# A hybrid decoder layer on eight cores: scratch in the staging tiles' layout, ones rows kept in the rings, and the first FFN norms spread among the gates

## The chip, the cores and the metric

The kernel runs on the eight cores of one Trainium2 chip. Core c works on sequence c//2 and on one half of its chunks (the odd or the even ones); no core waits for another. The time is that of the slowest core, in microseconds of the device. On each core five engines run their own in-order queues: TensorE (PE in the profile), ScalarE (ACT), VectorE (DVE), GpSimd (POOL) and SyncE (SP, which issues most of the DMAs).

## What is computed

One decoder layer on x of 4 x 8192 x 1024, cut to what matters:

```python
h = rmsnorm(x, g_mix_pre)
a_val, a_gate, q, k, v, f_logit = split(h @ w_in)          # 512 channels each, 8 heads for f
u = causal_depthwise_conv(a_val * sigmoid(a_gate))         # width 31
conv_out = silu(layernorm(u))
c = cumsum(log_sigmoid(f_logit + b_forget))                # per head
logits = q @ k.T / 8 + c[query] - c[key]                   # causal, 8 heads of 64
attn_out = softmax(logits) @ v
x = x + rmsnorm(concat(conv_out, attn_out) @ w_out, g_mix_post)
h = rmsnorm(x, g_ffn_pre)
y = (silu(h @ w_gate) * (h @ w_up)) @ w_down               # d_ff 2816
x = x + rmsnorm(y, g_ffn_post)
```

## The kernel before

**Chunks and streams.** A sequence has 16 chunks of 512 tokens. A core owns 8 of them (index j) and makes keys and values of all 16, of two chunks for each j. Three streams of work are recorded one into another by a small planner: `p_stream` (norms, K, V, Q, GLU gates, depthwise conv; until about 950 us), `f_stream` (output projection A1, first norm A2, second norm A3, then the FFN's up and down blocks; until the end), and `a_stream`, the attention, of which the planner mixes a share into both. The order of all instructions on each engine is fixed when the program is built: the planner counts the cost of what it has recorded (`fa`), and draws attention steps at a rate of at most 0.6 of the other work. A `yield ("att", d)` draws attention steps of d us by its own costs at that place, and they count against later ones.

**Dependencies.** Every operation names keys that it reads and writes (L77 on, `_record`). A DMA that writes a key waits for the last writer of that key and for its readers. Where that writer is another DMA, the wait stands on the issuing engine's queue, ahead of the instruction, until the earlier transfer has landed. The helpers `ld` (L345) and `st` (L349) give the keys of the whole buffer: `keys = buf.keys if keys is None else keys`. The key and value rings and the query rings are single-key buffers.

**Scratch.** K, V, q and the decay terms of a chunk pass through scratch tensors in device memory. Part 1 stores K twice: all of it in `k2_s` (per head 128 rows, key blocks of two halves on rows 0 to 63 and 64 to 127), and the half that the diagonal needs once more in `kd_s`, whose 68 rows per head hold 64 of K, one of ones and three of decay. `q_s` has 64 rows of q, one of decay, three of ones. Four stores at the start fill the ones rows.

**Attention loads.** A head (j, h) needs `s_qr` (q with its extra rows), `s_qw` (q again, on partitions 64 to 127) and `s_kd`; a unit (j, h, u) needs `s_kr` (K of chunk pair u) and `s_vr`. Heads have rings of `NQ = 3`, units of `NKV = 4`. `a_pump` (L1048) issues in turn the next head and the next unit as far as rings are free and stores are recorded, after each finished unit. All of these loads, the weights' loads of the FFN (`w_pump`), and the stores of K, q, V, u and conv stand on SP's one queue in that order; only the loads of x and u, and the conversion of the weights, are issued by POOL.

**First FFN norms.** `f_stream` (L989) at its start runs the conv's layernorm, gates 0 and 1 of the last own chunk (32 matmuls on `s_winG`), then A1(0) (64 matmuls on `s_wout`), A2(0) (whose statistics are two matmuls that read `s_hlA`), gates 2 and 3, A3(0) (two more of these matmuls), and attention of 3.0. Between the two statistics lie a chain on the other engines: the reciprocal root on ACT, eight residual steps of two instructions on DVE (L884, L886), eight squares, and their sum on POOL (L412, L428).

## Time and profile before

| | us |
|---|---|
| median of three runs (slowest core) | 2553.92 |
| the runs, from to | 2546.47 to 2798.3 |
| time of the profiled execution | 2545.8 |
| its span, core 6, the slowest | 2544.2 |
| spans of cores 0 to 7 | 2528.3, 2506.9, 2506.8, 2525.8, 2519.6, 2540.4, 2544.2, 2524.4 |
| PE busy | 2281.6 (90%) |
| ACT busy | 1576.0 (62%) |
| DVE busy | 1058.6 (42%) |
| POOL busy | 542.2 (21%) |
| DMA packets, bytes | 252408, 390.70 MB |

The span is that of the slowest core in one profiled execution; 1.6 us of its time lie outside of it. All cores do the same amount of work on the same addresses of their own, so differences between them are waits. SPq in a row is SP issuing a DMA; "landing" is the time from that issue to the last byte's arrival. "x16" counts instructions.

### The profile page before, as it was taken

Reading aid. Unit: us, or ns where it says so; the run is one execution under the profiler, and the core shown is the slowest. Engines: PE = TensorE matmul, PEld = TensorE weight load, DVE = VectorE, ACT = ScalarE, POOL = GpSimd, SP = SyncE. Lnnn points to the kernel's source line nnn. Section 1 sums busy time; section 2 is a strip of 40 time slices with the busy share of each in tenths; the row PEclk is TensorE's granted clock in tenths of the full one; section 3 lists DMA queues with packets and bytes.
Section 4 is the critical chain, followed back from the end, with each engine's and each line's share of the span. In section 5 each row is a group of like instructions: output and inputs, shape, how many; then the busy total and the mean of one; then the engine's idle time right before and its main releaser. Section 6 shows DMA issues by size and latency. Waiting matters only on the chain.

```text
span 2544.2 us, 52937 instructions; the slowest of 8 cores (2506.8 to 2544.2 us)
## 1 busy us (share of the span) xinstructions
PE 2281.6 (90%) x19680; PEld 1044.7 (41%) x19680; DVE 1058.6 (42%) x1640; ACT 1576.0 (62%) x1393; POOL 542.2 (21%) x901
## 2 busy tenths in 40 slices
PE   6888888889799869898999999999999999999895
PEld 2343334344344424344444444444444444444342
DVE  3545454434344443342424424424424342443643
ACT  2166566767577566676677777777767767772311
POOL 0231222121121240132023113113102202302301
PEclk9998899999899989999999999999999999998997
DMA  6996769597755956757635554654663463553542
GB/s 144 199 160 147 164 140 185 118 177 162 130 144 112 205 133 150 188 120 199 194 115 152 176 161 127 187 171 114 180 193 98 142 212 109 147 164 120 169 144 91
DMA packets 252408, 390.70 MB, mean 154 GB/s; under 512 B 29856, under 2 KB 182688, under 8 KB 252032
## 3 DMA queue, kind: packets, MB, share of 16 engines
q1 hardware_dynamic: 218928, 302.99, 43.9%
q0 software_dynamic: 33232, 84.34, 16.4%
q8 instruction: 164, 2.69, 0.5%
q14 instruction: 84, 0.69, 0.1%
HBM read 352.02 MB, written 77.20 MB: 169 GB/s over the span
## 4 chain that ended last, share of the span: by engine, by line
PE 65%; ACT 11%; issue 7%; DVE 6%; DMA 5%; SPq 3%; POOL 2%; DVEq 0%; ACTq 0%; POOLq 0%
PE pbig L375 65%; ACT s_pt L1097 5%; DMA s_kr<-k_s 2%; DVE s_tmp L884 2%; SPq L347 2%; DMA s_xs<-xT 1%; SPq L350 1%; ACT L387 1%; DVE s_x L886 1%; ACT s_sq L481 1%; ACT s_rstd L387 1%; ACT s_pt L1102 1%; DVE s_hT L468 1%; POOL s_ssA L412 1%; POOL s_pt L1106 1%
## 5 line engine op out<-in xcount | busy, mean ns | idle before, releaser
L1097 ACT ACTIVATE s_pt<-pbig,s_bias 128x2048 bf16<-128x2048 f32 x512 | 1005.7, 1964 | 448.1 <-PE pbig L375 445.3
L375 PE MATMUL pbig<-s_h,s_wr 128*128 128x512 bf16 x2816 | 694.3, 382 | 10.7 <-DVE s_sa L932 10.1
L375 PEld LDWEIGHTS pbig<-s_vr,s_pt 128*128 128x128 bf16 x8832 | 348.4, 98 | 174.1 <-issue 56.5
L375 PE MATMUL pbig<-s_vr,s_pt 128*128 128x65 bf16 x8832 | 369.9, 195 | 27.8 <-issue 8.6
L375 PE MATMUL pbig<-s_qr,s_kr 64*128 64x512 bf16 x1024 | 314.3, 387 | 81.3 <-ACT s_pt L1097 49.1
L375 PEld LDWEIGHTS pbig<-s_h,s_wr 128*128 128x128 bf16 x2816 | 243.7, 98 | 331.6 <-issue 112.5
L932 DVE SCALAR_TENSOR_TENSOR s_sa<-s_th,pbig 128x512 f32<-128x512 f32 x176 | 120.8, 686 | 488.1 <-ACT s_th L931 488.1
L375 PE MATMUL pbig<-s_qw,s_kr 64*128 64x512 bf16 x1024 | 315.7, 389 | 0.5 <-DMA s_qw<-q_s 0.5
L1106 POOL TENSOR_SCALAR_AFFINE_SELECT s_pt<-s_pt 128x128 bf16<-128x128 bf16 x256 | 86.5, 338 | 948.1 <-ACT s_pt L1102 922.8
L375 PE MATMUL pbig<-s_actA,s_wr 128*128 128x512 bf16 x1024 | 257.2, 381 | 1.7 <-DVE s_mix L965 1.1
L412 POOL TENSOR_TENSOR s_ssA<-s_ssA,s_sqr 128x512 f32<-128x512 f32 x112 | 153.0, 1366 | 449.3 <-ACT s_sqr L405 445.0
L375 PEld LDWEIGHTS pbig<-s_qr,s_kr 64*128 64x128 bf16 x1024 | 58.9, 94 | 293.2 <-issue 292.7
L375 PE MATMUL pbig<-s_hT,s_winKV 128*128 128x512 bf16 x512 | 146.0, 423 | 22.2 <-DVE s_hT L468 13.0
L931 ACT ACTIVATE s_th<-pbig 128x512 f32<-128x512 f32 x176 | 104.0, 591 | 87.3 <-PE pbig L375 82.1
L375 PE MATMUL pbig<-s_hT,s_winG 128*128 128x512 bf16 x512 | 134.6, 398 | 7.6 <-DVE s_ust L755 4.3
L375 PEld LDWEIGHTS pbig<-s_actA,s_wr 128*128 128x128 bf16 x1024 | 90.8, 98 | 122.6 <-issue 39.0
L375 PE MATMUL pbig<-s_winKV,s_hT 128*128 128x8 bf16 (+1 forms) x1024 | 139.7, 275 | 1.1 <-DVE s_vst L792 1.1
L412 POOL TENSOR_TENSOR s_ssV<-s_ssV,s_sqr 128x512 f32<-128x512 f32 x53 | 70.3, 1326 | 267.3 <-ACT s_sqr L405 267.1
L1102 ACT ACTIVATE s_pt<-pbig 128x1280 bf16<-128x1280 f32 x64 | 79.0, 1235 | 65.0 <-PE pbig L375 65.0
L884 DVE TENSOR_TENSOR s_tmp<-s_mix,s_rstd 128x512 f32<-128x512 f32 x120 | 97.6, 813 | 51.3 <-ACT s_rstd L389 51.3
L886 DVE SCALAR_TENSOR_TENSOR s_x<-s_tmp,s_vecs,s_x 128x512 f32<-128x512 f32 x120 | 112.0, 933 | 13.2 <-DVE s_tmp L884 0.5
L468 DVE SCALAR_TENSOR_TENSOR s_hT<-s_xs,s_vecs,s_rstd 128x512 bf16<-128x512 f32 x128 | 91.1, 745 | 34.9 <-ACT s_rstd L389 34.9
...
## 6 DMA issues: line engine op xcount, KB each, us to landing
...
s_wr<-wd_b SPq DMA_DIRECT2D x128, 352.0 KB, 3.2
s_vr<-v_s SPq DMA_DIRECT2D x288, 130.0 KB, 3.7
...
```

Source lines behind the costliest of these rows:

```text
L347: P.dma(q, lambda e: e.dma_start(out=out, in_=in_), reads=reads, writes=keys, sem=sem or buf.name)
L375: P.op("pe", lambda e: e.matmul(out, lhsT=lhsT, rhs=rhs, start=start, stop=stop, **kw), reads=reads, writes=[wkey])
L387: P.op("act", lambda e: e.activation(out=r[:, 0:ncol], in_=pb[b][:, 0:ncol], func=AF.Ln, bias=epsb[:, 0:1], scale=scale), reads=[PB(b)] + ...
L412: P.op(eng, lambda e: e.tensor_tensor(out=ss[:], in0=ss[:], in1=d[:], op=ALU.add), reads=ss.keys + d.keys, writes=ss.keys)
L468: return lambda: P.op("dve", lambda e: e.scalar_tensor_tensor(out=dst[:, k, :], in0=src[:, k, :], scalar=V(goff + k), in1=r[:], op0=ALU.mu ...
L884: P.op("dve", lambda e: e.tensor_tensor(out=T[:], in0=src[:, ob, :], in1=rstd[:], op=ALU.mult), reads=[src.keys[ob]] + rstd.keys, writes=T ...
L886: P.op("dve", lambda e: e.scalar_tensor_tensor(out=X[:, ob, :], in0=T[:], scalar=V(goff + ob), in1=X[:, ob, :], op0=ALU.mult, op1=ALU.add) ...
L931: P.op("act", lambda e: e.activation(out=T[:], in_=pb[bg][:], func=AF.Tanh, scale=0.5), reads=[PB(bg)], writes=T.keys)
L932: defer("ff", [lambda: P.op("dve", lambda e: e.scalar_tensor_tensor(out=A[:], in0=T[:], scalar=1.0, in1=pb[bg][:], op0=ALU.add, op1=ALU.mult),
L1097: P.op("act", lambda e: e.activation(out=p[:], in_=pbig[:, 0:4, :], func=AF.Exp, bias=bias[:, c, h:h + 1], scale=1.0), reads=bk + bias.key ...
L1102: P.op("act", lambda e: e.activation(out=p[:].rearrange("p a t -> p (a t)")[:, 0:1280], in_=pbig[:, 0:3, :].rearrange("p a t -> p (a t)")[ ...
L1106: P.op("pool", lambda e, ap=ap: e.affine_select(out=ap, in_=ap, pattern=[[1, 128]], base=0, channel_multiplier=-1, compare_op=ALU.is_ge, f ...
```

## The change

**Scratch.** `k2_s` and `kd_s` give way to one `k_s` (own index, 128 partitions, 4 head pairs, 2 halves, 512 tokens), whose row is what one partition of the staging tile holds: one store of 8 KB runs instead of eight. q, decay and V get tensors laid out in the same way (`q_s`, `c_s`, `v_s`), with one store each; the second copy of the diagonal half of K is no longer made. V's staging tiles grow to 12 blocks, so that the decayed copies lie in place, and `vst2` goes away; three small buffers of the conv's halo move behind `vst0`.

**Ones rows.** Six memsets on DVE fill rows 64 to 67 of the q and kd rings once; the four stores of ones are gone. A head is now loaded by five DMAs (q, its decay row, q again, kd, its three decay rows), K of a unit by two of 64 partitions each, with a semaphore each; V by one as before.

**First norms.** In `f_stream` A1(0) now comes ahead of the gates; gate 0 stands between A1 and A2, gates 1, 2 and 3 with attention of 1.0 behind each, and 2.0 more, between A2 and A3.

```diff
--- before.py
+++ after.py
@@ -208,12 +208,10 @@
     m32_d = dt_in("m32", [128, 32])
     yT_d = nc.dram_tensor("yT", [NOWN, 128, 8, CH], F32, kind="ExternalOutput").ap()
     scr = lambda name, shape: nc.dram_tensor(name, shape, BF16).ap()
-    k2_s = scr("k2_s", [NH, 128, S // 2])
-    kd_s = scr("kd_s", [NH + 1, 68, NOWN * CH])
-    q_s = scr("q_s", [NH + 1, 68, NOWN * CH])
-
-    kf, qf_ = kd_s.rearrange("h r t -> (h r) t"), q_s.rearrange("h r t -> (h r) t")
-    v_s = scr("v_s", [NH, 128, NOWN, 12, 65])
+    k_s = scr("k_s", [NOWN, 128, 4, 2, CH])
+    q_s = scr("q_s", [NOWN, 128, 4, CH])
+    c_s = scr("c_s", [NOWN, 4, 4, NH, 128])
+    v_s = scr("v_s", [128, NOWN, NH, 12 * 65])
     attn_s = scr("attn_s", [DATT, NOWN * CH])
     conv_s = scr("conv_s", [DCONV, NOWN * CH])
     u_s = scr("u_s", [NOWN, DCONV, UW])
@@ -301,10 +299,9 @@
     cst = BP("cst", [128, 128], BF16)
 
     OV = lambda name, shape, dt, over, parts=1, d=0: Buf(name, shape, dt, parts, [over.off + d])
-    vst = [OV("vst0", [128, NH, 8, 65], BF16, w4), OV("vst1", [128, NH, 8, 65], BF16, tmp[0])]
-    vst2 = OV("vst2", [128, NH, 4, 65], BF16, tmp[0], 1, 8320)
+    vst = [OV("vst0", [128, NH, 12, 65], BF16, w4), OV("vst1", [128, NH, 12, 65], BF16, tmp[0])]
     ust.append(OV("ust2", [128, CH], BF16, hlA, 1, 1024))
-    assert hlA.off + 1024 >= vst2.off + vst2.size and vst2.off >= vst[1].off + vst[1].size
+    assert hlA.off + 1024 >= vst[1].off + vst[1].size
 
     wout = Buf("wout", [128, 8, D], BF16, cur=[winKV.off], planes=4)
     mix = OV("mix", [128, 8, CH], F32, u4, 8)
@@ -556,23 +553,15 @@
 
         def decay(tb):
             def f():
-                o, ok = (W[:, :, 4 + tb, :], W.keys) if tb < 4 else (vst2[:, :, tb - 4, :], vst2.keys)
-                i_ = W[:, :, 4 + tb, :] if tb < 4 else W[:, :, tb - 4, :]
+                o, i_ = W[:, :, 4 + tb, :], W[:, :, tb + (4 if tb < 4 else -4), :]
                 P.op("dve", lambda e: e.tensor_tensor(out=o, in0=i_, in1=et3[:, tb, :].unsqueeze(2).to_broadcast([128, NH, 65]), op=ALU.mult),
-                     reads=W.keys + et.keys, writes=ok)
+                     reads=W.keys + et.keys, writes=W.keys)
             return f
-
-        def st_v():
-            st("sp", v_s[:, :, j, 0:8, :].rearrange("h p b d -> p h (b d)"), W[:].rearrange("p h b d -> p h (b d)"), W.keys, [("v_s", j, 0)], W.name)
-            st("sp", v_s[:, :, j, 8:12, :].rearrange("h p b d -> p h (b d)"), vst2[:].rearrange("p h b d -> p h (b d)"), vst2.keys, [("v_s", j, 1)], "vst2")
 
         def part4():
             flush("st")
-            for a in range(3):
-                st("sp", kd_s[0:NH, 65 + a, j * CH:(j + 1) * CH].rearrange("h (b t) -> b h t", t=128),
-                   cst[32 * a:32 * a + 32, :], cst.keys, [("c_s", j, a)], ("cst", a))
-            st("sp", q_s[0:NH, 64, j * CH:(j + 1) * CH].rearrange("h (b t) -> b h t", t=128), cst[96:128, :], cst.keys, [("c_s", j, 3)], ("cst", 3))
-            st_v()
+            st("sp", c_s[j].rearrange("a b h t -> (a b h) t"), cst[:], cst.keys, [("c_s", j)], "cst")
+            st("sp", v_s[:, j, :, :].rearrange("p h b -> p (h b)"), W[:].rearrange("p h b d -> p (h b d)"), W.keys, [("v_s", j)], W.name)
             ready[2 * j] = ready[2 * j + 1] = True
 
         nop = lambda: None
@@ -677,7 +666,7 @@
     u4h = (Buf("xh", [128, 8, HN], F32, 1, hcur), Buf("hh", [128, 8, HN], BF16, 8, hcur), Buf("sqh", [128, 8, HN], BF16, 8, hcur),
            None)
     assert hcur[0] <= u4.off + u4.size
-    hcur = [acc.off]
+    hcur = [vst[0].off + vst[0].size + 31 & ~31]
     u4h = u4h[:3] + (Buf("uh", [128, 4, HN], BF16, 1, hcur),)
     cwb = Buf("cwb", [128, 8, 16], F32, 1, hcur)
     m32 = Buf("m32", [128, 32], F32, 1, hcur)
@@ -696,9 +685,10 @@
         ld("sp", kmask, kmask[:], kmask_d)
         P.op("pool", lambda e: e.memset(ones_f[:], 1.0), writes=ones_f.keys)
         P.op("dve", lambda e: e.memset(carry[:], 0.0), writes=carry.keys)
-        P.op("dve", lambda e: e.memset(pt[0][:, 0:2, :], 1.0), writes=pt[0].keys)
+        for t in qring + kdring:
+            P.op("dve", lambda e, t=t: e.memset(t[64:68, :], 1.0), writes=t.keys)
         for W in vst:
-            P.op("dve", lambda e, W=W: e.memset(W[:, :, :, 64:65], 1.0), writes=W.keys)
+            P.op("dve", lambda e, W=W: e.memset(W[:, :, 0:8, 64:65], 1.0), writes=W.keys)
         P.op("dve", lambda e: e.tensor_scalar(out=V(V_HG, 8), in0=V(V_LNG, 8), scalar1=0.5, scalar2=None, op0=ALU.mult),
              reads=vecs.keys, writes=vecs.keys)
         norm_sq(0)
@@ -710,11 +700,6 @@
         yield from norm_fin(1)
         flush("h")
         load_x(2)
-        one = pt[0][0:96, 0:2, :].rearrange("p a t -> p (a t)")
-        st("sp", kd_s[0:NH, 64, :].rearrange("h (s t) -> h s t", t=1024), one[0:32, :], pt[0].keys, [("one", 0)], "one0")
-        st("sp", kd_s[NH, 0:12, :].rearrange("r (s t) -> r s t", t=1024), one[0:48, :], pt[0].keys, [("one", 2)], "one2")
-        st("sp", q_s[NH, 0:12, :].rearrange("r (s t) -> r s t", t=1024), one[0:48, :], pt[0].keys, [("one", 3)], "one3")
-        st("sp", q_s[0:NH, 65:68, :].rearrange("h r (s t) -> h r s t", t=1024), one, pt[0].keys, [("one", 1)], "one1")
         yield from p_kv(1)
         yield from norm_fin(2)
         flush("h")
@@ -772,14 +757,7 @@
                 yield from norm_fin(i + 2, i + 3)
 
         def st_k():
-            two = lambda t, o: t.rearrange("(hp two) r t -> two r hp t", two=2)[o]
-            for o in range(2):
-                K = kst[64 * o:64 * o + 64]
-                for a in range(2):
-                    st("sp", two(k2_s[:, 64 * a:64 * a + 64, j * CH:(j + 1) * CH], o), K[:, :, a, :, :].rearrange("p h b t -> p h (b t)"),
-                       kst.keys, [("k2", j, o, a)], ("kst", o, a))
-                    st("sp", two(kd_s[0:NH, 0:64, j * CH + 256 * a:j * CH + 256 * a + 256], o), K[:, :, a, 1, :],
-                       kst.keys, [("kd", j, o, a)], ("kstd", o, a))
+            st("sp", k_s[j].rearrange("p c a t -> p (c a t)"), kst[:].rearrange("p c a b t -> p (c a b t)"), kst.keys, [("k_s", j)], "kst")
         if own:
             defer("st", [st_k], 4)
         W, V0 = vst[min(j, 1)], 0 if own else 4
@@ -825,9 +803,7 @@
                 norm_sq(i + (1 if i == 3 else 2))
 
         def st_q():
-            for o in range(2):
-                st("sp", q_s[0:NH, 0:64, :].rearrange("(hp two) d t -> two d hp t", two=2)[o, :, :, j * CH:(j + 1) * CH],
-                   qst[64 * o:64 * o + 64, :, :], qst.keys, [("q_s", j, o)], ("qst", o))
+            st("sp", q_s[j].rearrange("p c t -> p (c t)"), qst[:].rearrange("p c t -> p (c t)"), qst.keys, [("q_s", j)], "qst")
             q_ready[j] = True
         defer("st", [st_q], 4)
         if not last:
@@ -994,14 +970,15 @@
         H = hT[(NCH - 1) % 3]
         bulk_flush("wo")
         yield from conv_ln(J - 1)
-        for cb in range(2):
-            yield from gates(J, cb, H)
         flush("c")
         yield from A1(0, range(8))
+        yield from gates(J, 0, H)
         yield from A2(0)
         w_pump()
-        for cb in range(2, 4):
+        for cb in range(1, 4):
             yield from gates(J, cb, H)
+            yield ("att", 1.0)
+        yield ("att", 2.0)
         yield from A3(0)
         yield ("att", 3.0)
         for j in range(NOWN):
@@ -1052,12 +1029,12 @@
                 j, h = heads[qn[0]]
                 if ready[2 * j + 1] and q_ready[j]:
                     r, w, kd = qring[qn[0] % NQ], qtwin[qn[0] % NQ], kdring[qn[0] % NQ]
-                    t = slice(j * CH, (j + 1) * CH)
-                    rq = [("q_s", j, 0), ("q_s", j, 1)]
-                    ld("sp", r, r[:], qf_[h * 68:h * 68 + 80, t], reads=rq + [("c_s", j, 3), ("one", 1), ("one", 3)])
-                    ld("sp", w, w[64:128, :], q_s[h, 0:64, t], reads=rq)
-                    ld("sp", kd, kd[:], kf[h * 68:h * 68 + 80, t],
-                       reads=[("kd", j, o, a) for o in range(2) for a in range(2)] + [("c_s", j, a) for a in range(3)] + [("one", 0), ("one", 2)])
+                    d = slice(64 * (h % 2), 64 * (h % 2) + 64)
+                    ld("sp", r, r[0:64, :], q_s[j, d, h // 2, :], reads=[("q_s", j)])
+                    ld("sp", r, r[67:68, :], c_s[j, 3:4, :, h, :], reads=[("c_s", j)], sem=r.name + "c")
+                    ld("sp", w, w[64:128, :], q_s[j, d, h // 2, :], reads=[("q_s", j)])
+                    ld("sp", kd, kd[0:64, :].rearrange("p (a t) -> p a t", a=2), k_s[j, d, h // 2, :, 256:512], reads=[("k_s", j)])
+                    ld("sp", kd, kd[64:67, :].rearrange("p (b t) -> p b t", b=4), c_s[j, 0:3, :, h, :], reads=[("c_s", j)], sem=kd.name + "c")
                     qn[0] += 1
                     did = True
             if un[0] < len(units) and un[0] < uf[0] + NKV:
@@ -1065,9 +1042,11 @@
                 if ready[2 * u + 1] and ready[2 * j + 1]:
                     kr, vr = kring[un[0] % NKV], vring[un[0] % NKV]
                     n = CH if u < j else CH // 2
-                    ld("sp", kr, kr[:, 0:n], k2_s[h, :, u * CH:u * CH + n], reads=[("k2", u, o, a) for o in range(2) for a in range(2)])
+                    d = slice(64 * (h % 2), 64 * (h % 2) + 64)
+                    for a in range(2):
+                        ld("sp", kr, kr[64 * a:64 * a + 64, 0:n], k_s[u, d, h // 2, a, 0:n], reads=[("k_s", u)], sem=(kr.name, a))
                     b0 = 4 if u < j else 0
-                    ld("sp", vr, vr[:], v_s[h, :, u, b0:b0 + 8, :], reads=[("v_s", u, 0)] + [("v_s", u, 1)] * (u < j))
+                    ld("sp", vr, vr[:].rearrange("p b d -> p (b d)"), v_s[:, u, h, b0 * 65:b0 * 65 + 520], reads=[("v_s", u)])
                     un[0] += 1
                     did = True
             if not did:
```

**The order on SP, the first attention loads.** Rows of the instruction order on SP before, where `a_pump` first runs: `s_kr`, `s_vr` and the numbers are ring buffers, and what stands in brackets is the semaphore that SP waits for ahead of the row.

```order
L347 DMA s_kr_49<-k_s 128x256
L347 DMA s_vr_53<-v_s 128x520 [waits p_ds_36]
L347 DMA s_qr_60<-q_s 80x512
L347 DMA s_qw_63<-q_s 64x512
L347 DMA s_kd_66<-kd_s 80x512
L347 DMA s_kr_50<-k_s 128x256
L347 DMA s_vr_54<-v_s 128x520
```

The same place after the change; each `p_ds` semaphore named here is that of the DMA in the row above, which writes the same buffer:

```order
L344 DMA s_qr_60<-q_s 64x512
L344 DMA s_qr_60<-c_s 1x4x128 [waits p_ds_39]
L344 DMA s_qw_63<-q_s 64x512
L344 DMA s_kd_66<-k_s 64x2x256
L344 DMA s_kd_66<-c_s 3x4x128 [waits p_ds_42]
L344 DMA s_kr_50<-k_s 64x256
L344 DMA s_kr_50<-k_s 64x256 [waits p_ds_44]
L344 DMA s_vr_54<-v_s 128x520
```

Sixteen issues in a row without a wait have become a queue in which the second half of each K load, and the decay rows of q and of kd, wait until the DMA ahead of them into that buffer has landed. There are 288 such waits for K and 128 for the heads in the program.

**The order on PE, ahead of A3(0).** Rows on PE before, up to the second statistics (`s_hlA`); `s_winG` are gate matmuls, the pairs of `s_qr` and `s_qw` with `s_kr` are attention scores of a unit, `s_kd` those of a diagonal, `s_vr` the values:

```order
L375 MATMUL pbig<-s_qr_59,s_kd_65 128x128
L375 MATMUL pbig<-s_qr_59,s_kd_65 128x256
L375 MATMUL pbig<-s_hT_80,s_winG 128x512 x4
L375 MATMUL pbig<-s_vr_54,s_pt_57 128x65 x16
L375 MATMUL pbig<-s_hT_80,s_winG 128x512 x4
L375 MATMUL pbig<-s_qr_60,s_kr_51 128x512
L375 MATMUL pbig<-s_qw_63,s_kr_51 128x512
L375 MATMUL pbig<-s_qr_60,s_kr_51 128x512
L375 MATMUL pbig<-s_qw_63,s_kr_51 128x512
L375 MATMUL pbig<-s_hlA,s_ones_bf 128x512 x2
```

And after:

```order
L372 MATMUL pbig<-s_identb,s_atok_71 128x128 x4
L372 MATMUL pbig<-s_qr_60,s_kr_52 128x512
L372 MATMUL pbig<-s_qw_63,s_kr_52 128x512
L372 MATMUL pbig<-s_qr_60,s_kr_52 128x512
L372 MATMUL pbig<-s_qw_63,s_kr_52 128x512
L372 MATMUL pbig<-s_vr_55,s_pt_58 128x65 x16
L372 MATMUL pbig<-s_qr_60,s_kr_52 128x512
L372 MATMUL pbig<-s_qw_63,s_kr_52 128x512
L372 MATMUL pbig<-s_qr_60,s_kr_52 128x512
L372 MATMUL pbig<-s_qw_63,s_kr_52 128x512
L372 MATMUL pbig<-s_vr_56,s_pt_57 128x65 x16
L372 MATMUL pbig<-s_hlA,s_ones_bf 128x512 x2
```

Between the two statistics stood 32 gate matmuls, three rounds of score matmuls off the diagonal and one on it; now 48 gate matmuls, seven rounds and one.

## Rows read from the trace of the kernel before

**Rows 1.** The page: the chain that ended last, by engine and line.

```profile
PE 65%; ACT 11%; issue 7%; DVE 6%; DMA 5%; SPq 3%; POOL 2%; DVEq 0%; ACTq 0%; POOLq 0%
PE pbig L375 65%; ACT s_pt L1097 5%; DMA s_kr<-k_s 2%; DVE s_tmp L884 2%; SPq L347 2%; DMA s_xs<-xT 1%; SPq L350 1%; ACT L387 1%; DVE s_x L886 1%; ACT s_sq L481 1%; ACT s_rstd L387 1%; ACT s_pt L1102 1%; DVE s_hT L468 1%; POOL s_ssA L412 1%; POOL s_pt L1106 1%
```

**Rows 2.** Waits of PE, core 6: releaser, us in total, times, longest.

```profile
PE pbig L375 <- POOL s_hlA L428: 17.8, 3, 12.3
PE pbig L375 <- DMA s_kr<-k_s: 17.8, 5, 7.0
PE pbig L375 <- issue: 17.1, 4, 6.6
```

**Rows 3.** Tile s_h, cores 1 and 6: ns min/median/max, first and last start.

```profile
L375 PE MATMUL pbig<-s_h,s_wr x2816: 376/379/634, 917.8 to 2440.4; 128*128 128x512 bf16 x188
...
L375 PE MATMUL pbig<-s_h,s_wr x2816: 376/379/634, 959.4 to 2477.8; 128*128 128x512 bf16 x188
```

**Rows 4.** Timeline of SP, core 6, first attention loads: start us, us, issue.

```profile
132.35 0.35 SPq L347 DMA_DIRECT2D s_qr<-q_s  x1
...
141.48 0.43 SPq L347 DMA_DIRECT2D s_vr<-v_s  x1
142.01 0.38 SPq L350 DMA_DIRECT2D u_s<-s_ust  x1
```

**Rows 5.** Tile s_kr, 130 to 199 us: own chunk 0's score matmuls.

```profile
L375 PE MATMUL pbig<-s_qr,s_kr x16: 376/386/603, 144.1 to 198.4; 64*128 64x512 bf16 x16
```

**Rows 6.** K loads' landing, core 6, windows 130:180, 334:540, 900:1000, 1200:1600.

```profile
DMA to landing us min/median/max: 5.7/8.3/12.6
...
DMA to landing us min/median/max: 2.1/5.7/22.2
...
DMA to landing us min/median/max: 2.4/3.0/5.1
...
DMA to landing us min/median/max: 2.0/3.6/7.9
```

**Rows 7.** K loads issued for own chunks 1 to 4: ns each, first, last.

```profile
L347 SPq DMA_DIRECT2D s_kr<-k_s x16: 337/521/2697, 186.0 to 332.4; - x16
...
L347 SPq DMA_DIRECT2D s_kr<-k_s x24: 320/522/2860, 335.9 to 538.1; - x24
...
L347 SPq DMA_DIRECT2D s_kr<-k_s x32: 319/442/4189, 546.0 to 818.4; - x32
...
L347 SPq DMA_DIRECT2D s_kr<-k_s x40: 319/428/7257, 820.9 to 1153.2; - x40
```

**Rows 8.** Timeline of SP's queue, core 6, behind the store burst of chunk 5.

```profile
648.73 6.95 SPq L347 DMA_DIRECT2D s_qr<-q_s  x1
...
657.36 4.19 SPq L347 DMA_DIRECT2D s_kr<-k_s  x1
```

**Rows 9.** DMA queue 1, 640:680, then 2320:2480: packets, MB, share of 16 engines.

```profile
q1 hardware_dynamic: 3811, 3.01, 50.7%
...
q1 hardware_dynamic: 7098, 22.37, 45.2%
```

**Rows 10.** Timeline of PE, core 6: the two statistics of the first norms.

```profile
921.98 0.58 PE L375 MATMUL pbig<-s_hlA,s_ones_bf 128*128 128x512 bf16 x1 [3.54 <-POOL s_hlA L428]
...
948.61 0.59 PE L375 MATMUL pbig<-s_hlA,s_ones_bf 128*128 128x512 bf16 x1 [12.26 <-POOL s_hlA L428]
```

**Rows 11.** Page, section 5: the gate matmuls (x512), busy us and mean ns.

```profile
L375 PE MATMUL pbig<-s_hT,s_winG 128*128 128x512 bf16 x512 | 134.6, 398 | 7.6 <-DVE s_ust L755 4.3
```

**Rows 12.** Waits and timeline of SP in the FFN stage, core 6.

```profile
SPq L163 <- PE pbig L375: 1216.7, 461, 14.4
...
1699.81 0.32 SPq L347 DMA_DIRECT2D s_kr<-k_s  x1
1705.00 0.32 SPq L347 DMA_DIRECT2D s_vr<-v_s  x1
```

**Rows 13.** Timeline of PE, core 6: the longest wait for a K load.

```profile
679.40 0.58 PE L375 MATMUL pbig<-s_qr,s_kr 64*128 64x512 bf16 x1 [6.98 <-DMA s_kr<-k_s]
```

## The prediction

> **What bounds the kernel now.** I read the page first, and in it the chain that ended last: two thirds of it are matmuls, and the largest item of a DMA is the wait for K loads, with SP's issues behind it [rows 1]. So PE sets the time, and a transfer matters where PE stands still for it. The list of PE's waits tells how much that is: 17.8 us on K loads, 17.1 us put down to "issue", in four pieces of up to 6.6 us, which I take to be loads too, and 17.8 us on the split of the sum of squares, nearly all of it at two places [rows 2, 10]. Next I compared cores. From the first FFN matmul on, cores 1 and 6 run alike (1522.6 and 1518.4 us to the last); before it core 6 is 41.6 us later [rows 3]. All that differs between cores lies in the first 960 us, where chunks are projected and stored. There the loads are slow: K lands after 8.3 us (median) in the first attention stretch, after 5.7 us between 334 and 540 us, but after 3.0 us in the quiet 900 to 1000 us and 3.6 us in the FFN stage [rows 6]. Behind a store burst the issue of a load alone takes 4.19 to 6.95 us [rows 8], and PE then waits up to 6.98 us for K [rows 13].
>
> **What the stores give.** One store per tensor replaces ten issues of K and q and six of decay and V, half a megabyte per chunk is not written twice, and rows grow to 8 KB. In the burst, queue 1 moves 3.01 MB in 3811 packets (0.79 KB each) with 50.7% of 16 engines over 40 us, which is 85 ns a packet and 9.3 GB/s an engine; with the weights' 3.15 KB packets it is 45.2% over 160 us for 22.37 MB, 163 ns and 19 GB/s [rows 9]. So long rows move about twice as fast, and bursts should at least halve. The ends of the gain are 0 (the two waits stay) and the 41.6 us by which core 6 lies behind core 1 [rows 3]; the K and issue waits sum to 34.9 us [rows 2]. I take 30. The Trainium skill ("DMA: Bandwidth & Descriptors", Specifications) puts the least transfer for full rate at 512 B, which the old rows already had; by that page the longer rows give nothing and the sum below would be 30 us higher. The trace speaks against it, with 9.3 and 19 GB/s on either side [rows 9].
>
> **What the loads cost.** The order on SP shows it: the second half of each K load waits for the landing of the first, and so do the decay rows of q and of kd, since they write one key. These are 288 and 128 landings, and everything on SP stands behind each. With L the time from issue to landing, and the issues at 0.35 to 0.5 us [rows 4], a unit now takes SP L + 0.8, a head 2L + 1.3. Before, three heads and four units went out from 132.35 to 141.91 us [rows 4], without a wait. Per stage:
> - own chunk 0 (8 heads, 8 units): 24L + 17, where SP had 66 us from the first issue to the last use [rows 4, 5];
> - chunk 1: 32L + 23 in the 150 us from its first K load to that of chunk 2 [rows 7];
> - chunk 2: 40L + 30 in 210; chunk 3: 48L + 36 in 275; chunk 4: 56L + 42 in some 334, its end with the FFN's weights.
>
> L is not in the trace: no load of half the rows, alone on its queue, is shown. Its ends are 2.4 us, the fastest quiet load, and 8.3 us, the first stretch [rows 6]. That 8.3 has four units in flight at once; now one transfer of SP is in flight, but xT and the weights' conversion share the engines. I take 4.5, nearer to the quiet 3.0 and the FFN's 3.6 than to the crowded stretch. Then chunk 0 takes 125 us for 66, 59 late; chunk 1 167 for 150, 17 late; chunks 2 to 4 fill 100, 92 and 88% of SP's time, and what bunches there (a head and two units after one release, stores between) I put at 8 us each, 24 in all, between 0 and 60. The stores of u, decay and V behind the first loads come late too, and the gates wait for their staging tiles; that falls into the same standstill. In the FFN stage SP waits 1216.7 us for PE over the run, and the next V load goes out 5.2 us after its K load, when PE frees the value buffer [rows 12]: a wait of 3.6 us for the first half ends inside it. I take 5 for the heads and weights there, between 0 and 40. Together 105.
>
> The Trainium skill (the same page, Rules for kernel authors) says of two transfers to disjoint partition halves: "Don't bother — they serialize", since both use the same 16 engines, and asks for one transfer of 128 partitions. That speaks against this edit, and by it the split has no gain to set against the waits; nothing is in the sum for one.
>
> **The first norms.** PE stands still for 3.54 us ahead of A2's statistics and for 12.26 us ahead of A3's [rows 10]. Between the two now lie 16 more gate matmuls, 6.4 us at 398 ns [rows 11], and four more rounds of scores with their values. That is enough to cover both, but attention drawn here is missing later. I take a gain of 10, between 3 and 15.8. In return A1(0) comes 32 gate matmuls earlier, 12.7 us, and may meet its weights and the last attention output on their way: 3, between 0 and 12.7.
>
> **Small things.** The four stores of ones and a memset go, six memsets of four rows come: nothing, since DVE is not in that place's wait. V's decay in place and the moved halo buffers change no instruction's size: nothing, unless a buffer is freed later, for which I have 5 as an upper end. After a stall matmuls take 0.58 us for the median's 0.38 [rows 3, 13]; some 40 of them after new stalls are 8 us, between 0 and 20.
>
> **The sum.** 2545.8 (the profiled execution) + 105 − 30 − 10 + 3 + 8 = 2621.8 us. The profiled time is 8.1 below the median of the runs, 2553.92, and no correction is made for that. 2% of the median, about what can be told from no change, is 51 us: faster ends at 2502.8, slower begins at 2605.0.
>
> **The rivals.**
> - **Half-loads land quickly, and the costs and gains cancel.** At L = 3.8 chunk 0 is 42 late, chunk 1 nothing (145 of 150), bunching 15 and the clock 4: 2545.8 + 42 + 15 + 4 − 30 − 10 + 3 = 2570. For it: a load of half as many rows, with smaller bursts beside it. Against: 5.7 and 8.3 in just these stretches [rows 6]. This ends and slower begins at L of about 4.3.
> - **The gain alone shows; faster.** One mechanism: the first half has landed by the time that SP would have had to wait for PE in any case, as in the FFN stage [rows 12], and the first stage keeps up. For 24L + 17 to fit into 66 us, L has to be 2.1 or less; at 2.4 it is 9 late. With that gone, the store term at its upper end and the norms at 10: 2545.8 − 41.6 − 10 + 3 = 2497; it decides at L of about 2.2. For it: loads have landed in 2.0 to 2.1 us now and then [rows 6]. Against: those are minima.
> - **The bursts stay.** The stores give nothing, as K still goes out in one piece ahead of the loads and holds the rings as long; then 2622 + 30 = 2652. Against it are the packet times [rows 9]. It is what the 512 B of the Trainium skill ("DMA: Bandwidth & Descriptors", Specifications) would make of the longer rows.
> - **The change doesn't do what it says for the norms.** The chain behind A2 is as long as before, and PE meets it later; 2632 instead of 2622. It is inside the forecast's range.
>
> **How the numbers follow.** I give the forecast 0.45, the bursts that stay 0.11, cancelling 0.34 and the gain alone 0.10. The predicted time is the first's, 2622. Its own range goes from 2605 to 2720: at L = 5.5 chunks 0 to 4 are 83, 49, 40, 25 and 16 late, 213 in all against 76, with the other terms 2748, and I go most of the way. The whole range has to take in most of the cancelling case, 2530 to 2605, and the lower end of that is where L is 3.0 (23 + 10 late, no clock; 2545.8 + 33 − 40 + 3 = 2542, less some 12 for the store term's other end). So 2530 to 2720. Slower is 0.45 + 0.11 = 0.56, same 0.34, faster 0.10.
>
> **What would show it.** In the new profile SP's waits have a row of DMA `s_kr`, `s_qr` and `s_kd` landings, some 416 in all, over 1000 us together; the first K load of chunk 1 goes out at about 250 instead of 186 us; PE has stalls behind DMA or "issue" between 144 and 330 us that sum to 60 or more; the first FFN matmul of core 6 is later than 959 us by 50 to 80, and cores lie closer together; from there to the end nothing changes by over 15 us; the 12.26 us at A3's statistics is below 6. The prediction is wrong if the new waits on SP last under 3 us each in the first 330 us, if PE doesn't wait there, or if the FFN stage becomes longer, which would mean that weights and stores behind the waits matter there too.

## The result, and the profile after

The change makes the kernel slower by far more than forecast: 2864.75 us, median of four runs, against 2565.54 for the kernel before on the same chip; ratio 1.1185, 95% interval 1.1076 to 1.1295. Forecast was 2622, with 2530 to 2720 as the range. The profiled execution took 2874.26 us, and its cores 2837.5 to 2871.7. Ratios here compare undisturbed runs only, while medians take in all; where the two differ, the ratio counts. The rows below are those of core 6, as before, unless another is named.

The chain that ended last, from the page (core 0), by engine and by line:

```profile
DMA 40%; PE 35%; SPq 11%; issue 5%; ACT 4%; DVE 4%; POOL 1%; DVEq 0%; ACTq 0%; POOLq 0%
PE pbig L372 35%; DMA s_kr<-k_s 23%; SPq L344 9%; DMA s_qr<-q_s 9%; DMA s_kd<-k_s 6%; ACT s_pt L1076 2%; DVE s_tmp L860 1%; SPq L347 1%; DMA s_cv<-conv_s 1%; DVE s_x L862 1%; ACT L384 0%; DMA s_xs<-xT 0%; DVE s_hT L465 0%; ACT s_rstd L384 0%; DMA wd_b<-w_down 0%
```

In [rows 1] matmuls were 65% and K loads 2% of it. Now DMA landings are 40% and the loads' issues by SP 9%: the path no longer runs along PE but along SP's queue and what it waits for. SP's own waits say it directly (releaser, us in total, times, longest):

```profile
SPq L161 <- DMA s_kr<-k_s: 1039.6, 288, 11.2
SPq L161 <- DMA s_qr<-q_s: 238.4, 64, 9.7
SPq L163 <- PE pbig L372: 189.4, 78, 10.1
SPq L161 <- DMA s_kd<-k_s: 182.9, 64, 10.5
```

These are the 416 landings of the prediction, 288 and twice 64, 1460.9 us together. What SP waited for PE has fallen from 1216.7 us [rows 12] to 189.4: over most of the run it is no longer PE that sets SP's pace. PE's waits now:

```profile
PE pbig L372 <- DMA s_kr<-k_s: 179.5, 47, 10.8
...
PE pbig L372 <- DMA s_cv<-conv_s: 40.2, 5, 13.9
...
PE pbig L372 <- DVE s_ust L740: 23.7, 3, 20.0
...
PE pbig L372 <- DMA s_qr<-c_s: 11.8, 4, 5.7
...
PE pbig L372 <- POOL s_hlA L425: 2.0, 1, 2.0
```

K loads cost PE 179.5 us where they cost 17.8 [rows 2]; the conv outputs' load for A1 (`s_cv`), behind the waits in the same queue, another 40.2, the u stores (through their staging tiles `s_ust`) 23.7, of which 20.0 in one piece. POOL's part of the wait for the split of the squares, 17.8 us before [rows 2], is down to 2.0. Where in the run it was lost is told by the first and last FFN matmul:

```profile
L372 PE MATMUL pbig<-s_h,s_wr x2816: 376/379/634, 1106.3 to 2785.8; 128*128 128x512 bf16 x188
```

The first comes at 1106.3 us for 959.4, so 146.9 of core 6's loss lie ahead of it; from there to the last one it is 1679.5 us for 1518.4 [rows 3], another 161.1. And a single landing isn't slow. For all K loads, issue to landing:

```profile
DMA to landing us min/median/max: 2.0/3.0/11.6
```

The median is 3.0 us, that of the quiet stretch before, where the first stretch had 8.3 [rows 6].

### The profile page after: what moved, and what is told of

Same layout as the page of the kernel before. It is cut to its first block, busy times and chain, and to the rows that moved or that the text cites. A ratio compares the mean times of both kernels' runs of the same rounds, so it can differ in the third digit from the quotient of the medians.

```text
span 2871.7 us, 53550 instructions; the slowest of 8 cores (2837.5 to 2871.7 us)
## 1 busy us (share of the span) xinstructions
PE 2356.3 (82%) x19680; PEld 1068.8 (37%) x19680; DVE 1066.8 (37%) x1645; ACT 1578.2 (55%) x1393; POOL 539.9 (19%) x901
## 3 DMA queue, kind: packets, MB, share of 16 engines
q0 software_dynamic: 33232, 84.34, 14.3%
## 4 chain that ended last, share of the span: by engine, by line
DMA 40%; PE 35%; SPq 11%; issue 5%; ACT 4%; DVE 4%; POOL 1%; DVEq 0%; ACTq 0%; POOLq 0%
PE pbig L372 35%; DMA s_kr<-k_s 23%; SPq L344 9%; DMA s_qr<-q_s 9%; DMA s_kd<-k_s 6%; ACT s_pt L1076 2%; DVE s_tmp L860 1%; SPq L347 1%; DMA s_cv<-conv_s 1%; DVE s_x L862 1%; ACT L384 0%; DMA s_xs<-xT 0%; DVE s_hT L465 0%; ACT s_rstd L384 0%; DMA wd_b<-w_down 0%
## 5 line engine op out<-in xcount | busy, mean ns | idle before, releaser
L372 PE MATMUL pbig<-s_h,s_wr 128*128 128x512 bf16 x2816 | 714.2, 391 | 18.2 <-DVE s_sa L908 17.5
L372 PE MATMUL pbig<-s_qr,s_kr 64*128 64x512 bf16 x1024 | 324.3, 397 | 287.3 <-DMA s_kr<-k_s 221.4
L372 PEld LDWEIGHTS pbig<-s_vr,s_pt 128*128 128x128 bf16 x8832 | 358.5, 100 | 173.6 <-issue 62.8
L372 PE MATMUL pbig<-s_vr,s_pt 128*128 128x65 bf16 x8832 | 379.6, 197 | 17.3 <-DVE s_atok L1116 8.5
L372 PE MATMUL pbig<-s_qw,s_kr 64*128 64x512 bf16 x1024 | 325.9, 400 | 2.7 <-DMA s_qw<-q_s 2.7
L912 DVE SCALAR_TENSOR_TENSOR s_actA<-s_sa,pbig 128x512 bf16<-128x512 f32 x128 | 87.7, 685 | 63.0 <-PE pbig L372 54.1
```

What stands on the lines that cost most here:

```text
L372: P.op("pe", lambda e: e.matmul(out, lhsT=lhsT, rhs=rhs, start=start, stop=stop, **kw), reads=reads, writes=[wkey])
L912: P.op("dve", lambda e: e.scalar_tensor_tensor(out=actT(f), in0=A[:], scalar=0.5, in1=pb[bu][:], op0=ALU.mult, op1=ALU.mult), reads=A.keys ...
```

## The experiments

All times are medians in us; a ratio is to the kernel before, run on the same chip. The last two columns are core 6's first FFN matmul in the profiled run, and the time from there to its last one.

| run | what it is | time | ratio (95%) | first FFN | FFN |
|---|---|---|---|---|---|
| before | | 2565.54 | 1 | 959.4 | 1518.4 |
| the change | | 2864.75 | 1.1185 (1.1076 to 1.1295) | 1106.3 | 1679.5 |
| e1 | no waits on landings | 2523.88 | 0.9841 (0.9778 to 0.9905) | 926.6 | 1520.4 |
| e2 | K waits only | 2637.35 | 1.0273 (1.0205 to 1.0341) | 992.0 | 1576.2 |
| e9 | head waits only | 2605.09 | 1.0148 (1.0083 to 1.0214) | 997.1 | 1527.2 |
| e3 | waits for own chunks 4 to 7 | 2725.25 | 1.0601 (1.0506 to 1.0696) | 955.3 | 1686.9 |
| e5 | waits for own chunks 0 to 3 | 2669.88 | 1.0469 (1.0401 to 1.0536) | 1085.0 | 1515.4 |
| e6 | all waits, V between the K halves | 2784.09 | 1.0882 (1.0804 to 1.0961) | 1069.0 | 1620.4 |
| e8 | before, with split K loads | 2781.12 | 1.062 (1.0523 to 1.0718) | 1045.0 | 1580.8 |
| e4 | no waits, K as one transfer | 2544.35 | 0.993 (0.9902 to 0.9958) | 930.0 | 1516.4 |
| e7 | e1 with the old norms' order | 2571.55 | 0.9892 (0.9811 to 0.9973) | 916.2 | 1524.8 |
| e10 | e4 with K by head in scratch | 2522.44 | 0.9855 (0.9803 to 0.9906) | 918.2 | 1515.0 |
| e11 | before, with the new norms' order | 2557.07 | 0.9995 (0.9962 to 1.0028) | 967.9 | 1518.1 |

e1, e4, e7 and e10 lie below both kernels, by 0.7 to 1.6%, and none of their intervals reaches 1.

**e1, the waits taken away.** The rings of K, q and kd get a second key for the second transfer, and each load writes its own (of q and kd the decay rows have the second); PE, which reads both keys, waits for both landings. No transfer, address or size changes.

```diff
-    kring = [B(f"kr{i}", [128, CH], BF16) for i in range(NKV)]
+    kring = [B(f"kr{i}", [128, CH], BF16, planes=2) for i in range(NKV)]
...
-                        ld("sp", kr, kr[64 * a:64 * a + 64, 0:n], k_s[u, d, h // 2, a, 0:n], reads=[("k_s", u)], sem=(kr.name, a))
+                        ld("sp", kr, kr[64 * a:64 * a + 64, 0:n], k_s[u, d, h // 2, a, 0:n], reads=[("k_s", u)], sem=(kr.name, a), keys=[kr.keys[a]])
```

> Every transfer of the changed kernel stays, but the two halves of a K load, and q or kd and their decay rows, have a key each, so the 416 waits of SP on landings are gone. Theory W (the waits hold up all that stands behind them on SP): the whole loss goes and the gains of stores and norms show, 2490 to 2540 us. Rival D (the transfers themselves: halves of 64 partitions, 256 B rows, 288 + 128 more of them, or the new layout's addresses): the loss stays for the most part, above 2750 us. A time between, 2600 to 2700, would mean that both count.

Measured 2523.88: the whole loss of some 340 us was the waits, and without them the change is 1.6% faster than the kernel before (0.95 to 2.2%). Theory W holds; D, by which halves of 64 partitions and 256 B rows would be dear in themselves, falls, since all of them are still there.

**e2 and e9, one kind of wait at a time.** Each has half of e1's edit: in e2 q and kd have two keys and K has one, in e9 K has two (`planes=2`, `keys=[kr.keys[a]]`) and q and kd one.

> Only the 288 K waits stay (1053 of 1494 us of landing waits in the changed kernel's profile), the 128 of the heads are gone. Theory W as a saturated queue: SP needs about 5.1 us a unit and 3 a head, 293 us for own chunk 5 where the stage lasted 318, so SP keeps up but for bunches and the time falls by far more than the heads' share of the waits: 2560 to 2640. Theory W as latency (each wait costs PE its share): 2865 - 0.3 x 340 = 2760. D: 2830 or more.

> The counterpart of the second run: only the 128 head waits stay (441 of 1494 us), the 288 K waits are gone. If loss is proportional to wait: 2523.9 + 0.3 x 341 = 2625. If it is what SP cannot absorb (theory W as a filled queue): SP needs 1.5 us a unit and 10 a head, about 150 us for own chunk 5 where the stage lasts 318, so only own chunks 0 and 1 are short of time: 2530 to 2565. The two halves would then cost 113 and some 20 apart and 341 together.

e2 at 2637 is within what the filled queue gives, with 113 us over e1. (The expectation's 5.1 us a unit and 3 a head give 269 us for own chunk 5 and not 293; either is less than the 318 of the stage.) e9 is a miss: 2605, some 80 us over e1, where 10 to 40 were expected. Its first and last FFN matmul show where:

```profile
L372 PE MATMUL pbig<-s_h,s_wr x2688: 376/379/634, 997.1 to 2524.3; 128*128 128x512 bf16 x192
```

From 997.1 to 2524.3 are 1527.2 us, 6.8 more than in e1: in the FFN stage the head waits cost next to nothing, as expected. All else, 70.5 us, lies ahead of it, where heads follow each other after one to four units and SP has to bring many of them at once. The first V load of own chunk 1 goes out 47 us later than in e1 (235.9 for 188.6), that of chunk 2 58 later (392.6 for 334.2): most of the loss is chunk 0's. So the place was foreseen and the size was not. Together 113 and 80 would be 193; the change lost 341. The two kinds don't add, as they would not if each uses up slack that the other needs; the count of one stage below bears that out.

**e3 and e5, one stage at a time.** The same keys as in e1, but where the condition holds both loads write both keys, and so the second waits: `j >= 4` in e3, `j < 4` in e5 (q, kd and their decay rows in the same way).

```diff
-                        ld("sp", kr, kr[64 * a:64 * a + 64, 0:n], k_s[u, d, h // 2, a, 0:n], reads=[("k_s", u)], sem=(kr.name, a))
+                        ld("sp", kr, kr[64 * a:64 * a + 64, 0:n], k_s[u, d, h // 2, a, 0:n], reads=[("k_s", u)], sem=(kr.name, a), keys=kr.keys if j >= 4 else [kr.keys[a]])
```

> All waits stay for own chunks 4 to 7 (attention from about 820 us on), none for chunks 0 to 3. In the prediction's working the FFN stage hides them, which gives 2520 to 2560. By the profile after, in which the first FFN matmul is some 160 us later and the rest another 160 us longer, it is 2660 to 2700, with the first FFN matmul of the slowest core below 980 us.

> The counterpart of the third run: waits for own chunks 0 to 3 only (80 units, 32 heads), none for 4 to 7. Theory W with the prediction's stage formula at the landing that the profile after shows (about 3.7 us of wait a landing): chunk 0 about 50 late, chunk 1 some 20, then bunching: the first FFN matmul some 80 to 130 us later than without waits, 2600 to 2650. If the two halves of the loss simply add to the full loss (341 us, of which the FFN's half was 201): 2523.9 + 140 = 2664. The FFN stage itself as without waits (about 1522 us from first to last FFN matmul).

e3 is the run that decides against the prediction's step, by which it would have taken 2520 to 2560; it also lies above the 2660 to 2700 that the profile after had led to. With waits only from own chunk 4 on, the first FFN matmul of core 6 comes at 955.3 us, 28.7 after e1's (chunk 4 starts at about 800 us, so part of that is chunk 4's), and the FFN takes 1686.9 us for 1520.4. e5 is the mirror: 1085.0, and an FFN of 1515.4. Its first FFN matmul is 158 us later than e1's where the stage formula gave 80 to 130, and 2670 is above the formula's 2600 to 2650, next to the 2664 of a plain sum. By the ratios e3 loses 7.6% of the kernel before's time to e1 and e5 6.3%, the change 13.4%: 13.9 for 13.4. Stage by stage the losses add; kind by kind, 4.3% and 3.1% for the same 13.4, they do not.

**e6, the same waits with V's issue inside.** One line moved: the V load goes out between the two K halves.

```diff
+                    b0 = 4 if u < j else 0
                     for a in range(2):
                         ld("sp", kr, kr[64 * a:64 * a + 64, 0:n], k_s[u, d, h // 2, a, 0:n], reads=[("k_s", u)], sem=(kr.name, a))
-                    b0 = 4 if u < j else 0
-                    ld("sp", vr, vr[:].rearrange("p b d -> p (b d)"), v_s[:, u, h, b0 * 65:b0 * 65 + 520], reads=[("v_s", u)])
+                        if a == 0:
+                            ld("sp", vr, vr[:].rearrange("p b d -> p (b d)"), v_s[:, u, h, b0 * 65:b0 * 65 + 520], reads=[("v_s", u)])
```

> The changed kernel with all 416 waits, but the V load of a unit is issued ahead of the second K half instead of behind it, so its issue of about 0.5 us falls into the wait. Nothing else moves. If SP's time is what bounds the kernel (theory W, saturated queue): 288 x 0.5 = 144 us of SP time less over a stage that SP fills, so 80 to 150 us faster than the change, 2715 to 2785. If what costs is the length of each load's chain (two landings one after the other): V comes a little earlier, K as late as before, 2840 to 2865. D: no change.

2784 is 81 us faster than the change, 77 by the ratios (1.0882 for 1.1185): at the edge of the lower range and clear of the rival's 2840. All 416 waits are there still, and K's second half goes out no sooner after its first, 4.2 us on average in both runs; what got shorter is SP's time for a unit. V comes earlier too, which the rival priced at 0 to 25 us. So most of the gain is SP's time.

**e8, the split alone.** The kernel before, with each K load in two halves that write one key.

```diff
-                    ld("sp", kr, kr[:, 0:n], k2_s[h, :, u * CH:u * CH + n], reads=[("k2", u, o, a) for o in range(2) for a in range(2)])
+                    for a in range(2):
+                        ld("sp", kr, kr[64 * a:64 * a + 64, 0:n], k2_s[h, 64 * a:64 * a + 64, u * CH:u * CH + n], reads=[("k2", u, o, a) for o in range(2)], sem=(kr.name, a))
```

> The kernel before, whole, with one edit: each K load is issued as two transfers of 64 partitions that write one key, so 288 landing waits on SP and no other part of the change. W: as in the second run, where these waits cost 113 us over the run without them, and more since the store bursts are still there: 2660 to 2720. If the cost came from the new layout together with waits: 2600 or less.

Ratio 1.062: on the 2549.22 of the kernel before on its chip that is 2707, within the expected range, and 158 us of loss. So the waits need nothing of the new scratch to cost what they do; with the new scratch the same 288 cost 113 (e2). Why they cost less there isn't shown; the expectation put it down to the store bursts.

**e4 and e10, K in one transfer.** Without waits the split itself may still cost. e4 joins the halves by an access:

```diff
-                    for a in range(2):
-                        ld("sp", kr, kr[64 * a:64 * a + 64, 0:n], k_s[u, d, h // 2, a, 0:n], reads=[("k_s", u)], sem=(kr.name, a))
+                    ld("sp", kr, kr[:, 0:n], k_s[u, d, h // 2, :, 0:n].rearrange("p a t -> a p t"), reads=[("k_s", u)])
```

e10 joins them by another layout of the scratch, into which K is stored by four DMAs of 64 x 4 x 512:

```diff
-    k_s = scr("k_s", [NOWN, 128, 4, 2, CH])
+    k_s = scr("k_s", [NOWN, NH, 2, 64, CH])
...
+                    ld("sp", kr, kr[:, 0:n], k_s[u, h, :, :, 0:n].rearrange("a d t -> (a d) t"), reads=[("k_s", u, o, a) for o in range(2) for a in range(2)])
```

> As the first run, and K of a unit is one transfer of 128 partitions again, read from the new layout by an access of two halves. W: SP issues 288 transfers of 0.45 us less, but is not what PE waits for: within 15 us of the first run, 2485 to 2530. D: a gain of 30 us or more over the first run.

> No waits, and K in scratch by head, 128 rows of 1 KB each, so that a K load is one transfer of 128 partitions with 128 rows in a line, as in the kernel before; the store becomes four of 64 x 4 rows of 1 KB. q, decay, V and the ones rows are as in the change. If the run with one K load per unit lost its 20 us because its access started with a dimension of two halves, this one has not that loss: 2505 to 2530. If 288 fewer issues were bad in themselves, or the 1 KB store rows cost what long rows gained: 2540 or more.

e4 was expected within 15 us of e1, or 30 and more faster, and is 20 slower: both readings missed. The joined load has no landing in the profile, but the V load, which goes out right behind it, has: between 1200 and 1600 us on the slowest core of each (count, size, median us to landing), first e4, then e1:

```profile
s_vr<-v_s SPq DMA_DIRECT2D x59, 130.0 KB, 5.5
```

```profile
s_vr<-v_s SPq DMA_DIRECT2D x60, 130.0 KB, 3.1
```

It lands after 5.5 us behind a joined K load, after 3.1 behind two halves. e10 has one transfer of 128 rows in a line, and is as fast as e1 (0.9855 to 0.9841, each inside the other's interval). So neither one transfer nor two is dear; e4's access is. The Trainium skill ("DMA: Bandwidth & Descriptors", Rules for kernel authors) says why that may be: the outermost dimension of an access sets over how many engines a DMA is spread, and e4's, on the side of device memory, is 2. The runs agree with it but don't show the engines.

**e7 and e11, the norms.** e7 is e1 with the old `f_stream` order, which this undoes; e11 is the kernel before with the new one.

```diff
         flush("c")
         yield from A1(0, range(8))
-        yield from gates(J, 0, H)
         yield from A2(0)
         w_pump()
-        for cb in range(1, 4):
+        for cb in range(2, 4):
             yield from gates(J, cb, H)
-            yield ("att", 1.0)
-        yield ("att", 2.0)
         yield from A3(0)
```

(Gates 0 and 1 stand ahead of the `flush` again.)

> The first run without waits, with the old order of gates, A1, A2 and A3. By the prediction's term for the norms (10 us gained, 3 lost by A1 being earlier) it is 7 us slower than that run, 2531; rival: the norms' order is worth the whole 40 us of that run's gain, 2560; or nothing, 2524.

> The kernel before with the new order of gates, A1, A2, A3 alone. By the prediction's term 7 us faster than before, ratio 0.997; at the term's ends 0.994 and 1.004. Rival: the norms are worth 20 us or more, ratio 0.992 or less.

Alone the new order gives 0.9995 (0.9962 to 1.0028): no gain that can be measured, and at most 10 us. The 7 us net that were forecast lie inside that interval, the rival's 20 do not. e7's ratio, 0.9892, can't be told from e1's 0.9841 either. Yet PE's wait has gone, as its waits between 860 and 960 us show, first in e7, then in e1:

```profile
PE pbig L372 <- POOL s_hlA L425: 15.4, 2, 11.8
PE pbig L372 <- ACT s_pt L1075: 4.3, 4, 1.8
```

```profile
PE pbig L372 <- ACT s_pt L1076: 18.6, 11, 6.4
```

Of the 15.4 us that `s_hlA` gives up, 14.3 come back as waiting for ACT's exponentials (`s_pt`). The kernel before and e11 show the same between 880 and 970 us: 15.8 us of `s_hlA` go, and `s_pt` rises from 9.3 to 32.1. The timeline of PE in e1 has the place, ahead of A3's statistics at 914.14 us (start, us, what, idle before):

```profile
896.65 1.23 PE L372 MATMUL pbig<-s_qr,s_kd 68*128 68x512 bf16 x4 [6.39 <-ACT s_pt L1076]
...
911.88 0.58 PE L372 MATMUL pbig<-s_qr,s_kr 64*128 64x512 bf16 x1 [1.21 <-ACT s_pt L1076]
...
914.14 0.63 PE L372 MATMUL pbig<-s_hlA,s_ones_bf 128*128 128x512 bf16 x1 [0.22 <-issue]
```

And ACT's timeline says what the 6.39 us are:

```profile
892.56 0.63 ACT L402 ACTIVATE s_sqr<-s_x 128x512 f32<-128x512 f32 x1 [2.72 <-DVE s_x L862]
893.10 0.58 ACT L736 ACTIVATE s_th<-pbig 128x512 f32<-128x512 f32 x1
894.02 0.63 ACT L402 ACTIVATE s_sqr<-s_x 128x512 f32<-128x512 f32 x1 [0.34 <-DVE s_x L862]
894.55 1.95 ACT L1076 ACTIVATE s_pt<-pbig,s_bias 128x2048 bf16<-128x2048 f32 x1
```

The exponential that PE waits for starts at 894.55 us, behind squares of the norm (L402) that wait in ACT's queue for the residual on DVE, 2.72 us for one alone. PE no longer waits for the chain of the norm itself, but for an exponential that stands in one queue with it. That is the longest of the 11 waits; several of the others, like the 1.21 us at 911.88, stand between rounds of attention with nothing else between them, where PE waits for the exponential itself, 1.97 us a piece.

## Why the prediction was wrong

**The mechanism was right; the first stage's number came near by luck.** 416 landing waits on SP were forecast, "over 1000 us together": 1460.9. K of own chunk 1 was forecast to start at about 250 us: it goes out at 254.52. Chunk 0 was put 59 us late, and the first V load of chunk 1 comes at 257.77 for 188.80, 69 later. L, the landing that was guessed at 4.5, was not too low: a wait is 3.6 us on average for K (1039.6 by 288), 3.7 for q and 2.9 for kd, behind issues of 0.45 to 0.61. In the first stage it was too high. SP's waits in the first 330 us:

```profile
SPq L161 <- DMA s_kd<-k_s: 38.5, 12, 9.2
SPq L161 <- DMA s_qr<-q_s: 34.1, 12, 5.0
SPq L161 <- DMA s_kr<-k_s: 32.5, 13, 5.8
```

These are 37 waits of 2.8 us on average, below the 3 that the prediction had named as a sign of being wrong. At 2.7 us of wait, the average from 130 to 258 us, behind an issue of 0.5, its 24L + 17 gives 94 us, 28 late and not 69. And PE's waits for loads between 144 and 330 us are 21.9 us (`s_qr` 11.8, `s_qw` 7.6, `s_kd` 2.5) where 60 or more were named; its longest there is the 20.0 us behind a u store, which stands on SP behind the loads of three heads and four units and goes out at 171.25 us. The formula counts attention loads alone. How the other 41 us divide among the stores in that queue and PE's standstills isn't shown.

**The step that failed is the FFN stage: "a wait of 3.6 us for the first half ends inside it. I take 5".** It should have been some 160: 161.1 against the kernel before, 159.1 against e1. The prediction's own sign for this, the FFN stage becoming longer, is what came. A head, three units and two weights' loads follow each other there on SP without a gap, in the profile after (start, us, issue; x2 of K holds the wait between the halves):

```profile
1500.24 0.64 SPq L344 DMA_DIRECT2D s_qr<-c_s  x1
1500.93 0.47 SPq L344 DMA_DIRECT2D s_qw<-q_s  x1
1501.45 0.61 SPq L344 DMA_DIRECT2D s_kd<-k_s  x1
1504.89 0.77 SPq L344 DMA_DIRECT2D s_kd<-c_s  x1
1505.71 3.16 SPq L344 DMA_DIRECT2D s_kr<-k_s  x2
1509.03 0.47 SPq L344 DMA_DIRECT2D s_vr<-v_s  x1
1509.60 0.85 SPq L344 DMA_DIRECT2D s_wr<-wd_b  x2
1510.49 4.59 SPq L344 DMA_DIRECT2D s_kr<-k_s  x2
1515.14 0.57 SPq L344 DMA_DIRECT2D s_vr<-v_s  x1
1515.81 3.59 SPq L344 DMA_DIRECT2D s_kr<-k_s  x2
```

The row that I took for cover, 5.2 us between a K and a V load [rows 12], is SP waiting for PE to free the value buffer. That time is slack, but SP has only so much of it, and each stage has its own. For own chunk 5 it can be counted. Without waits on landings (e1) its stage goes from 1130 to 1449 us, 319 us, in which SP waits for PE:

```profile
SPq L163 <- PE pbig L372: 152.7, 71, 4.8
```

With them it goes from 1332 to 1718 us, 386 us, and SP waits:

```profile
SPq L161 <- DMA s_kr<-k_s: 178.5, 48, 7.5
SPq L161 <- DMA s_qr<-q_s: 33.4, 8, 8.3
SPq L161 <- DMA s_kd<-k_s: 19.6, 8, 4.3
...
SPq L163 <- PE pbig L372: 1.1, 1, 1.1
```

231.5 us of new waits against 152.7 us of slack leave 78.8, and the stage is 67 us longer. (SP also waits 10.1 us for DVE's residual in e1's stage, and no longer after, which leaves 69.) With K waits alone they are 180.0 us, 27 over, and that stage of e2 took 350 us, 31 more; with the heads' alone (e9) 45.1 us, which fits in: SP still waits 110.9 us for PE there, and the stage took 327 us, 8 more. The prediction had the formula for this and applied it to chunks 0 to 4 only. For chunk 5, 8 x 6 units and 8 heads at L = 3.6 give 48 x 4.4 + 8 x 8.5 = 279 us, 87% of the stage's 319 ahead of any weights, and at the L of 4.1 that came (3.6 of wait behind an issue of 0.45) it is 311: a queue that is full before the weights' loads and the output's stores. I argued from one unit (a wait of 3.6 inside a gap of 5.2) instead of from the sum of a stage. e3 shows the term by itself, 1686.9 for 1520.4, and e6 that most of it is time on SP and not the latency of single loads: there a wait for K is 3.0 us (151.5 by 51) for the 3.7 above (178.5 by 48), and slack comes back, in 1300 to 1700 us:

```profile
SPq L161 <- DMA s_kr<-k_s: 151.5, 51, 6.2
...
SPq L163 <- PE pbig L372: 22.1, 12, 4.6
```

**The term for chunks 0 to 4 was half of what came.** Forecast were 59, 17 and three times 8 us, 100 in all. By the first V load of each next chunk, the stages of own chunks 0 to 4 end 69, 93, 126, 129 and 171 us later than before, but in that the stores' gain is taken off, which the prediction has as a term of its own. Against e1, which has the same stores, they end 69, 101, 141, 171 and 202 us later, so they add 69, 32, 40, 30 and 31: 202 for 100, the last one partly in the FFN stage. Chunks 1 to 4 were all low; the slack of their queue was put too high, or the bunching too low, and the runs don't split the two. e5 with waits for chunks 0 to 3 alone moves core 6's first FFN matmul by 158.4 us against e1. So of the 339 us between e1 and the change on core 6, 180 lie ahead of the first FFN matmul and 159 behind it, where 100 and 5 were forecast. The upper end of the forecast doesn't cover it either: its 213 us for L = 5.5 give 2759 with the sum's other terms, or 2735 without the bunching, not 2748.

**The clock's term was too small.** 8 us were forecast; PE is busy 2375.2 us for 2281.6, 94 more, with the same matmuls. The granted clock (after the times of PEld, DVE, ACT and POOL, ahead of the DMA share) between 144 and 330 us and in the FFN, after the change:

```profile
144.00:330.00 186.00, 126.51 (x942) 56.88 (x940) 61.43 (x115) 80.27 (x83) 31.96 (x71) 0.76 0.42 105
1106.00:2786.00 1680.00, 1493.71 (x12359) 677.50 (x12357) 598.34 (x870) 999.26 (x818) 304.33 (x362) 0.95 0.48 139
```

The kernel before, between 144 and 330 us and in its FFN:

```profile
144.00:330.00 186.00, 153.85 (x1434) 72.44 (x1433) 82.69 (x151) 114.09 (x117) 49.47 (x120) 0.91 0.79 160
959.00:2478.00 1519.00, 1449.26 (x12430) 664.32 (x12428) 597.55 (x871) 1004.63 (x821) 304.21 (x362) 0.99 0.53 155
```

Means of 0.76 and 0.95, for 0.91 and 0.99 before, are more time at the lower of the two levels, 1.2 of 2.4 GHz, which matmuls after a standstill show (0.58 us for 0.38 [rows 3, 13]); K loads alone stop PE 47 times for 5 [rows 2]. The FFN alone has 44 us more of busy PE for it. How much of that the time shows is open: the count of SP's queue in own chunk 5 comes out without it.

**The gain of the stores was the right size; its reason is shown in part.** 30 us were forecast, out of long rows. Without the waits and with the old norms (e7) the gain is 1.1% (0.3 to 1.9%), 28 us, with the new (e1) 1.6%, and e1's first FFN matmul on core 6 comes 32.8 us earlier than before; e11 puts nothing of it down to the norms. K's row length isn't the reason. Queue 1 between 130 and 930 us (packets, MB, share of 16 engines' time), before, in e1 (K's rows of 8 KB) and in e10 (1 KB, as K's main store had before):

```profile
q1 hardware_dynamic: 85656, 69.39, 40.8%
```

```profile
q1 hardware_dynamic: 61910, 66.25, 31.1%
```

```profile
q1 hardware_dynamic: 66275, 67.23, 29.2%
```

e10's K goes out in rows of 1 KB and costs as little as e1's. What both have less of is packets, 62 and 66 thousand for 86: gone are the second copy of K's diagonal half with its rows of 512 B, the rows of ones, and V's rows of 1040 and 520 B, which are 12.5 KB long now, in e10 too. (The decay's rows of 256 B have stayed.) V's long rows may have paid: in the same window its store lands sooner, before (the first of its two stores) and then in e1 (count, size, median us to landing),

```profile
v_s<-s_vst SPq DMA_DIRECT2D x7, 1040.0 KB, 13.0
```

```profile
v_s<-s_vst SPq DMA_DIRECT2D x7, 1560.0 KB, 7.3
```

and K's does not:

```profile
k_s<-s_kst SPq DMA_DIRECT2D x24, 256.0 KB, 11.7
```

```profile
k_s<-s_kst SPq DMA_DIRECT2D x6, 1024.0 KB, 13.2
```

No run separates these, so the prediction's reason is refuted for K and open for V. The rival of the bursts that stay is refuted by e7's and e1's gain, and by e1's waits of PE:

```profile
PE pbig L372 <- DMA s_kr<-k_s: 8.1, 3, 3.9
...
PE pbig L372 <- issue: 3.2, 17, 0.3
```

"Issue" is 3.2 us for 17.1; with the old stores it stays at 15.2 in e11. K loads cost 8.1 for 17.8, but e11 has 9.7 as well, so that drop says little. The Trainium skill's least size of 512 B ("DMA: Bandwidth & Descriptors", Specifications), which the prediction set aside, fits K's store in e10 so far as it goes: from 1 KB to 8 KB nothing is gained.

**The norms gave nothing that can be measured**, where 10 were forecast, less 3: the mechanism was seen (the statistics wait for 2.0 us), what comes next wasn't, ACT.

**The rival of the halves that land quickly** had the landing nearly right: 3.8, where 4.1 came on average for K and 4.5 was taken. Even so the result was slower than every case: what was missed was how many landings a stage can take, not how long one is.
